# Second norm's rows of blocks 0 and 1 turned by VectorE in 32x32 pieces, and one weight split put four tiles earlier, in a hybrid attention and ConvGLU block

## What is computed

```python
h = rms_norm(h_res, norm1_g)                       # first norm
proj = h @ w_in                                    # q 512, k 128, v 128, p 512 columns
a = sliding_window_sink_attention(rms_norm(q), rms_norm(k), v, attn_sinks)
m = multiscale_pool(p, pool_w, pool_b, pool_scale) # windows 2, 4, 8, 16
h_res = h_res + concatenate([a, m]) @ w_out
h2 = rms_norm(h_res, norm2_g)                      # second norm
h_res = h_res + conv_glu(h2, w_up, conv_w, conv_b, w_down)
```

## Time and profile before

| what | value |
|---|---|
| median of 3 runs | 1779.94 us (1777.8 to 1780.89) |
| the profiled execution | 1777.87 us, span 1776.1 us |
| TensorE busy | 1755.0 us, 99% of the span |
| VectorE busy | 1334.2 us, 75% |
| ScalarE busy | 805.2 us, 45% |
| GpSimd busy | 241.1 us, 14% |
| granted TensorE clock over the span | 1.000 |
| DMA | 321.73 MB, mean 181 GB/s |

### The profile page before, as it was taken

One profiled execution on the slowest core, in us unless ns is written; L12 is line 12 of the kernel. 1 busy time (PEld: TensorE's weight loads), 2 busy tenths in 40 slices (PEclk: granted clock), 3 DMA queues, 4 the chain that ended last, 5 costly groups with the idle time before them and its releaser, 6 DMA issues.

```text
span 1776.1 us, 23434 instructions
## 1 busy us (share of the span) xinstructions
PE 1755.0 (99%) x8490; PEld 1462.4 (82%) x8490; DVE 1334.2 (75%) x1796; ACT 805.2 (45%) x1437; POOL 241.1 (14%) x270
## 2 busy tenths in 40 slices
PE   7999999999999999999999999999999999999999
PEld 6888888888878888888888888888888888888887
DVE  5645634535779999999998998998998777865874
ACT  4554544534755444444454444444444433333321
POOL 1213212202110000000000000000003022220210
PEclk9999999999999999999999999999999999999999
DMA  8563383484445523423366223223227999976884
GB/s 313 224 229 108 105 318 111 166 290 155 164 170 181 204 84 116 145 83 95 119 241 221 72 83 96 71 84 95 72 83 245 337 339 334 310 254 209 304 286 131
DMA packets 211555, 321.73 MB, mean 181 GB/s; under 512 B 13737, under 2 KB 106097, under 8 KB 211441
## 3 DMA queue, kind: packets, MB, share of 16 engines
q1 hardware_dynamic: 192014, 267.75, 45.1%
q10 hardware_dynamic: 19427, 52.49, 7.6%
HBM read 249.93 MB, written 70.25 MB: 180 GB/s over the span
## 4 chain that ended last, share of the span: by engine, by line
PE 89%; DVE 4%; DMA 3%; ACT 2%; issue 1%; SPq 1%; POOL 0%; ACTq 0%; DVEq 0%; POOLq 0%
PE ps L810 28%; PE ps L812 28%; PE ps L811 28%; DMA rw<-in_w_up_dram 1%; PE ps L969 1%; PE ps L993 1%; DVE wv L1745 1%; PE ps L980 1%; PE ps L1033 1%; DMA raw<-in_w_out_dram 1%; DMA raw<-in_w_in_dram 1%; DVE hT_lo L1564 0%; DMA gT_d<-cb 0%; DVE va_lo L1788 0%; POOL ss_q L2043 0%
## 5 line engine op out<-in xcount | busy, mean ns | idle before, releaser
L810 PE MATMUL ps<-va_hi,wv 128*128 128x512 f32 x1232 | 479.9, 390 | 1.4 <-DVE va_lo L1751 0.8
L811 PE MATMUL ps<-va_lo,wv 128*128 128x512 f32 x1232 | 479.3, 389 | 0.0
L812 PE MATMUL ps<-va_hi,wv 128*128 128x512 f32 x1232 | 479.3, 389 | 0.0
L810 PEld LDWEIGHTS ps<-va_hi,wv 128*128 128x128 f32 x1232 | 231.3, 188 | 51.1 <-issue 2.3
L812 PEld LDWEIGHTS ps<-va_hi,wv 128*128 128x128 f32 x1232 | 231.3, 188 | 48.2
L811 PEld LDWEIGHTS ps<-va_lo,wv 128*128 128x128 f32 x1232 | 231.3, 188 | 47.9
L810 PE MATMUL ps<-dt_hi,ds_hi 128*128 128x512 f32 x616 | 239.6, 389 | 0.0
L811 PE MATMUL ps<-dt_lo,ds_hi 128*128 128x512 f32 x616 | 239.6, 389 | 0.0
L812 PE MATMUL ps<-dt_hi,ds_lo 128*128 128x512 f32 x616 | 239.6, 389 | 0.0
L1838 DVE SCALAR_TENSOR_TENSOR cb<-ub,cst,cb 128x1024 f32<-128x1024 f32 x176 | 220.8, 1298 | 9.7 <-ACT cb L1357 9.7
L1357 ACT ACTIVATE cb<-ub,cst 128x1024 f32<-128x1024 f32 x88 | 108.9, 1244 | 142.6 <-DVE ub L1893 86.3
(11 more groups left out here) (170 smaller groups left out, 2844.5 us busy)
## 6 DMA issues: line engine op xcount, KB each, us to landing
dg<-gT_d SPq DMA_DIRECT2D x264, 256.0 KB, 5.3
rw<-in_w_up_dram SPq DMA_DIRECT2D x84, 512.0 KB, 5.0
dw<-in_w_down_dram SPq DMA_DIRECT2D x132, 256.0 KB, 5.4
gT_d<-cb ACTq DMA_DIRECT2D x44, 512.0 KB, 2.6
raw<-in_w_out_dram SPq DMA_DIRECT2D x32, 512.0 KB, 4.1
w_hi<-wA_d SPq DMA_DIRECT2D x30, 512.0 KB, 3.3
w_lo<-wA_d SPq DMA_DIRECT2D x30, 512.0 KB, 4.8
n<-in_x_dram SPq DMA_DIRECT2D x16, 512.0 KB, 8.0
```

Source lines behind the costliest of these rows:

```text
L810: pe.matmul(out_ap, l_hi, r_hi, start=first, stop=False, skip_group_check=True)
L811: pe.matmul(out_ap, l_hi, r_lo, start=False, stop=False, skip_group_check=True)
L812: return pe.matmul(out_ap, l_lo, r_hi, start=False, stop=last, skip_group_check=True)
```

## The change

Two edits. TensorE's part of `t2` is empty for blocks 0 and 1, and VectorE has one in its place. It turns two tiles at a time: 16 transposes, each of 32 partitions by 256 elements, from piece (m, n) of the source to piece (n, m) of the two PSUM banks. The first of a pair waits for the copies of the pair before (or, for j = 0, for the bank to be free and the rows to be scaled), and the last counts both tiles as turned. ScalarE's part, the banks and the list stay as they are. The other edit puts `split(1)` behind the fourth turned tile of block 0 in place of the eighth, on ScalarE and on VectorE.

```diff
             def t2(a, j):
+                if a < NB - 2:
+
+                    return
                 for dt in (2 * j, 2 * j + 1):
                     if dt >= t2_lag(a):
                         pe.wait_ge(S["h2_copied"], KT * a + dt - t2_lag(a) + 1)
-                    elif a + 2 < NB:
-                        pe.wait_ge(S["p_copied"], 4 * (a + 2) + dt + 1)
...
-                    if a == 0 and i == KT - 1:
+                    if a == 0 and i == 3:
                         split(1)
...
+            def t2(a, j):
+                if a >= NB - 2:
+
+                    return
+
+                if j:
+                    dve.wait_ge(S["h2_copied"], KT * a + 2 * j)
+                else:
+                    dve.wait_ge(S["p_copied"], 4 * (a + 2) + 2)
+                    dve.wait_ge(S["xs2"], NT * a + NT)
+                src = rows[a][:, :, 2 * j * P:(2 * j + 2) * P].rearrange("p t (e c) -> p e t c", e=2)
+                b = t2_bank(a, 0)
+                dst = ps[:, b:b + 2, :].rearrange("p e (t c) -> p e t c", t=NT)
+                for m in range(4):
+                    for n in range(4):
+                        tr = v.transpose(dst[32 * n:32 * n + 32, :, :, 32 * m:32 * m + 32],
+                                         src[32 * m:32 * m + 32, :, :, 32 * n:32 * n + 32])
+                tr.then_inc(S["turned2"], 2)
...
-                    if a == 0 and i == KT - 1:
+                    if a == 0 and i == 3:
                         split(1)
```

More of the change, by code:

```diff
@@ L1826, in _ @@
             walk(dict(n1=n1_, n1sc=n1sc, t1=t1, win=win, pin=pin, pl=pl, o=o, q=q, qn=qn, kv=kv, kve=kve, join=join, s=s, inv=inv, inv1=inverse, av=av,
-                      n2sc=n2sc, first_weights=first_weights, va=va, va3=va3))
+                      n2sc=n2sc, t2=t2, first_weights=first_weights, va=va, va3=va3))
             def tap(un, s, j):
```

## The result

| | before | after |
|---|---|---|
| median, us | 1779.05 (1777.8 to 1780.89, 4 runs) | 1815.31 (1814.34 to 1818.48, 4 runs) |
| ratio | | 1.0204 [1.0191, 1.0216] |
| profiled execution, us | 1777.87, span 1776.1 | 1814.38, span 1812.6 |
| granted clock over the span | 1.000 | 0.99 |

The kernel is slower by 36.3 us, or by 36.5 us from one profiled execution to the other. The direction was forecast with 0.91, but the time was not: 1815 lies above the whole range, 1786 to 1807. The forecast of 1797 started from the median of three executions, 1779.94; with the fourth it is 1779.05.

What follows compares the result with a forecast made beforehand. TensorE was taken to bound the kernel. The turning, 8X - 26.25 = +18.5 us over both blocks, less 1.5 for the split gave +17: 1779.94 + 17 = 1797 us, range 1786 to 1807.

Steps and rivals of the forecast that it cites:

- What bounds the kernel, and TensorE's share: TensorE is busy 99% of the span; eight transposes take 0.87 us, so it can give back 7.0 us in all.
- The price of a transpose: On VectorE, 0.35 us each between bounds 0.26 and 0.42, so a call of 16 takes X = 5.6 us.
- each pays in full: Rival: every VectorE transpose costs as if alone, X = 6.7 us or more, giving 1806 us; chance 0.14.
- The chain in block 0: Four calls and ScalarE's copies alternate; `pm(2, 0)` waits for the last copy, at 246.85 + 4X; cost 4X - 13.5 = +8.9 us.
- The first wait's end: `kv(2, 0)` waits for the `carry` behind the first pair's copies until 244.2; its 3.7 us are not added.
- Block 1: The same chain one block later, ending at `pm(3, 0)`: 4X - 12.75 = +9.65 us.
- The clock: Rival: TensorE's clock falls to 1.2 GHz behind each wait at `pm`, 5.5 us more each, 1808 us; chance 0.05.
- the other cases: Forecast 0.60, dense transposes 0.12, each in full 0.14, cover enough with no change 0.04, or faster 0.05.
- The split: Earlier `split(1)` delays `pin(0, 1)` by 0.9 us but frees ScalarE's queue, shortening TensorE's 2.56 us `carry` wait: -1.5 us.

Runs made afterwards that it cites:

- the experiment: No layer computed: VectorE alone, 16 instructions each of 14 kinds, 256 elements, varying the partition group: 0.33 us each on a fixed group, 0.46 or 0.47 where it changes.
- the last kernel: Against before: VectorE turns pairs 1 and 3, TensorE 2 and 4, with the split, `carry` ahead of first copies, pair 4's copies ahead of `kve`: 1774.3 us, ratio 0.9979.
- the added products: Kernel after with 12 products adding zeros on TensorE ahead of `pm` in blocks 2 and 3: 1811.11 us, ratio 1.0187.

## Why the prediction was wrong, by its steps

**What bounds the kernel, and TensorE's share**: right. The whole loss is time in which TensorE stands or runs at half clock.

**The price of a transpose: the step that failed.** I took 0.35 us between 0.26 and 0.42, and held the row of 0.34 for the nearest "with a little for a kind of instruction that the trace lacks". Measured is 0.469, above even my upper bound of 0.42, the row of one such instruction alone; one transpose of the kernel's form is listed with 0.456 at the median. The row chosen has the right number of elements and the wrong neighbours: it and the one ahead of it are on the same partitions and overlap, while the pieces of a turning go from group to group and don't. It counts 128 times: 8 x (7.5 - 5.6) = +15.2 us. The rival "each pays in full", X = 6.7 or more, came nearest: 1779.94 + 33.75 - 1.5 = 1812 us with X = 7.5. Its reason fell, though, since transposes on a fixed group overlap as other instructions do. Of the Trainium skill I weighed two figures from "The TRN2 errata", 0.33 and 0.39 us, and passed by the section on held instructions (quoted with the experiment). Both are too low for a turning, though 0.33 is what the rows on a fixed group give. With it the row to take would have been that of an instruction alone, 0.42 us, and the center of the forecast my upper bound, still 0.05 us a transpose short. The rule under "Rules for kernel authors", to turn 128x128 on TensorE, was borne out by the price, 7.5 us a pair against 0.87, and for this change; the last kernel shows that two pairs a block on an idle VectorE pay all the same.

**The chain in block 0**: right. From the end of `cat_lo` to `pm` it says 10.75 + 4X, with X = 7.5 that is 40.75 us. Measured: 275.98 - (233.78 + 1.28) = 40.92. The first wait's end, forecast at 244.2, becomes 245.05 with the measured X and the 1.05 us that `cat_lo` came earlier; the row says 244.99. That it adds nothing was shown by the run with the `carry` moved.

**Block 1**: right as well. The same step gives 40.75, and 41.2 were measured (`pm(3, 0)` at 418.95, `cat_lo` at 376.25 + 1.50).

**The clock: a rival that came true beside the forecast.** I gave it 0.05, since the page showed full clock behind the wait of 7.8 us at the start. That argument was weak (the last section), and so was setting the clock against the other cases. `pm(2, 0)` is 15.6 us late and the group at line 956 is 18.7 us late, so 3.1 us are lost between them; in block 1 it is 35.15 against 36.8, so 1.7 us (the clock was back after 3 us there). That is 4.8 us where the rival had 11. Both `pm` dates of before are the prediction's own estimates, 260.36 and 383.8; TensorE's timeline of before has them at 260.23 and 383.67, which makes the losses 3.0 and 1.5 us, 4.5 together, and moves 0.3 us from this term to the chain. The Trainium skill's sentence on the idle state at half rate (TensorE: Matmul & The Clock Gate, "Part 1"), which I set aside for the row, agrees with what after shows: 0.50 behind both waits at `pm`. The same page, "HAM oscillation", tells of kernels that lose time in this way, behind each wait of TensorE anew; here the part behind `pm` is what the added products gave back, 3.4 us by the traces. It wasn't an alternative to the other cases, to be weighed against them, but an addition to every case with a wait long enough.

**The split**: right in sign and path, too small in size. Against the profiled execution it is 1.05 us in `cat_lo` (233.78 against 234.82), 0.45 less than the 1.5. Against the medians it is 3.3 us, or 2.6 on top of the turning, of which part is open.

**The sum again**, against the profiled execution: 17 + 15.2 (price) + 4.8 (clock) + 0.45 (split) = 37.5 us; 36.5 were measured. The 1.0 us left over is about what `cat_lo` of block 1 gained on the group ahead of it (17.45 us late against 18.7). The traces show where: in both kernels VectorE waits for the DMA `x_d<-r` there, starts scaling the rows (353.03 before, 370.25 after), and `cat_lo` follows 6.00 us behind that start. So `cat_lo` of block 1 hangs on a load that came only 17.2 us later, and not on TensorE. Why the load came so, no run looked for.

**The range.** Its upper end rested on one idea of the worst case, each instruction alone, and on a chance of 0.05 for the clock. Both ends of X should have come from rows of unlike kinds, and the clock's loss belonged in the upper end of all cases that hold a wait.

## What to carry to other kernels

Price an instruction by a row that has not only its size but its neighbours: what stands ahead of it, and on which partitions; where no such row exists, one short kernel with VectorE alone gives it. Idle time on an engine isn't room for work that is handed over in small pairs through a shared bank: here 30 us of transposes became 40.9 us of chain, and two fixed dates (the `carry`, `pm`) hung on it. Split such work so that each engine does its part in one run, put what others wait for ahead of it in each queue, and add to the price of a long wait on TensorE the slow work behind it.

## What the runs showed of the hardware

- **VectorE's overlap is lost with a change of the group of 32 partitions.** Transposes into PSUM take 0.33 us each for 256 elements on a fixed group, 0.46 to 0.47 when source or target group changes; 16 copies into PSUM take 5.31 and 6.98 us. The number of partitions, 32, 64 or 128, makes no difference. I had not expected it, though the section of the Trainium skill on held instructions, named with the experiment, has it.
- **TensorE's granted clock read 0.50 behind waits of 3.08, 3.51, 5.4 and 13.2 us, and 1.00 behind 2.56 and 2.68.** Behind such a wait the lower level lasted for 3 to 6 us of work.
- **The clock column doesn't show it everywhere.** The argument from the start of the kernel was read from that column alone. The windows of the kernel before at its start:

```profile
9.00:10.00 1.00, 1.00 (x7) 0.94 (x6) 0.28 (x2) 0.68 (x2) 0.83 (x3) 1.00 1.15 347
...
12.00:13.00 1.00, 1.00 (x12) 1.00 (x11) 0.61 (x3) 0.20 (x1) 0.00 (x0) 1.00 0.23 57
```

Both read a clock of 1.00, and yet the same transposes go 7 in a microsecond behind the wait and 12 later on; 21 of them take 4.44 us, 0.21 each, where eight take 0.87 in the earlier trace rows. So there is a slow stretch behind the wait of 7.8 us too, of the kind seen behind `pm`. Whether it is the clock can't be told from this column. The instructions' own pace is the surer reading, and it would have given the rival its due.
